# Moving two operand splits between weight pairs 1 and 2, and two output tiles within the last weight pair, in a hybrid encoder step

## The chip, the cores and the metric

The kernel runs on 1 core of one Trainium2 chip. The metric is the device time in microseconds of one execution, lower is better. Times are the median of several runs, and one further execution was profiled.

## The reference, cut to what matters

One layer of a hybrid encoder is computed for 1024 prompt tokens and 64 sample tokens, T = 1088 in all, at width 1024:

```
h = RMSNorm(x);  [u | v_g | q | k | v | g] = h @ w_in
A = gMLP chunked spatial gating of u and v_g
B = sliding-window attention with ALiBi and sinks, 16 q heads, 4 kv heads
x = x + w_o( sigmoid(g_A) * (A @ w_pa) + sigmoid(g_B) * (B @ w_pb) )
x = x + w_down( gelu(causal_dwconv3(h2 @ w_up_gate)) * (h2 @ w_up_val) ),  h2 = RMSNorm(x)
y = RMSNorm_final(x)
```

Outputs are y for all tokens and the new cache rows. Everything is float32. Each float32 operand is split in two fp32r parts, high and low, and a product is three passes over them: high by high, high by low, low by high.

## The kernel before, in words

All big matrix products run through 64 **weight pairs** p = 0 to 63 (two column tiles of 128 columns each, all 8 K-tiles), and what is left of w_down through a last part of its own. The moving operand, the activations, lies in SBUF as four quadrants (even or odd K-tiles, first or second 544 tokens). A pair is either **plain**, 8 products of quadrants, or a **Strassen-like** pair of 7 products on sums of quadrants. Pairs 0 and 1 are plain, pair 2 is the first with 7 products. One product is 4 K-tiles j by 3 passes by 2 halves of 272 tokens, 24 matmuls (line 2395).

The operands of the sums are numbered: 0, 1, 6 and 7 are the quadrants, 2, 3, 4 and 5 are sums. The plain pairs use 0, 1, 7 and 6; pair 2 uses 0 to 6 in that order, so operand 4 is first needed by its product k = 4 and operand 5 by k = 5. An operand is **split** in two steps: ScalarE writes `op_hi`, a copy of all 128x2176 elements rounded to fp32r (`operand_hi`, line 1288), and VectorE writes `op_lo`, the source less the high part (`operand_lo`, line 1730). In the first generation of operands (g = 0) operand 4's high part goes over the source of operand 5, so `operand_hi(0, 4)` waits until `op_lo` of 5 has been written.

Weights are treated alike: `raw` (one buffer) holds the pair's weights as loaded, ScalarE writes `w_hi` (line 1249), VectorE `w_lo` (line 1686), and in a 7-product pair VectorE first makes four sums of blocks (`weight_sum`, lines 1697, 1702, 1706, 1710). The order in which VectorE makes the low parts of pair 2 is places 3, 0, 1, 4 in pair 1 and, at the start of pair 2, the ones `left_over`: 2, 5, 6.

What is done when is written out by hand. Every engine runs the same loop over (p, k, j), product k of pair p and its K-tile j, and in each step issues what tables say belongs there. In a plain pair the product k has a slot number n: k = 0, 1, 3, 4, 5, 6, 7 is n = 0 to 6 and k = 2 has none; tables with (n, j) go by that. In a 7-product pair n = k. Engines wait for one another by semaphores and each works its own list strictly in order. The steps around the change, in the order of the lists:

- ScalarE, pair 1, k = 7 (n = 6), j = 0: copy of a finished quadrant out of PSUM, copy of v (`values(1)`, line 1345), then `operands` (line 1288), then the high part of pair 2's weight place 1; j = 1: that of place 4. Pair 2, k = 0, j = 0: the last quadrant of pair 1, high parts of places 2, 5, 6; j = 1: operand 5's high part (before); j = 3: `load_weights(act, 3)`; k = 1, j = 0: `copied(2, 0)`, which takes the first product of pair 2 out of PSUM into `m1c` (line 1336); then `values(2)` and, before, operand 4's high part.
- `load_weights(engine, p)` (line 613) issues two DMAs into `raw` and first waits for `s_w >= LOWS_BEFORE[p]`: for p = 3 that is until VectorE has made all low parts of pairs 0 to 2, since these read `raw`.
- VectorE, pair 1, k = 7: low part of place 1, the distance table (lines 1932 to 1936), low part of place 4, the fourth weight sum (line 1710, at j = 2). Pair 2, k = 0, j = 0: low parts of places 2, 5, 6; j = 2: operand 5's low part (before); k = 1, j = 2: operand 4's low part; k = 2: `combine(2, Q11)`.
- TensorE starts product k = 2 of pair 2 only when `copied(2, 0)` is done, since it writes the same PSUM region.

The last part of w_down works on 3 chunks of tokens: 512, 384 and 192 of them (`CHUNKS`), and 8 column tiles kt each, 6 matmuls per tile (line 2660). VectorE adds each to the residual (line 2308). Once a chunk is summed, its token tiles n (0 to 3, 4 to 6, 7 and 8) are **turned**: 8 transposes on TensorE (line 2642) into one of two PSUM places used in turn, a sum of squares on ScalarE (line 1653), the factor on GpSimd (lines 1117, 1120), and then **scaled** on VectorE into the output rows (line 2298), which SyncE stores. Tile n's transposes wait until tile n - 2 is scaled (tiles 2 to 6), those of tiles 7 and 8 until the third chunk is summed. `TURNS[c]` says behind which kt of chunk c TensorE turns a tile, `SCALES[c]` behind which kt VectorE scales one. A matmul group kt of the last two chunks waits for the addition four groups earlier, whose bank it takes.

Of the kernel before, what the change touches and what calls it, by code (L numbers as in the profile page):

```python
# [121 lines left out]

GROUPS = FT // 2 - 4 * NCHUNK
CHUNKS = ((0, 4), (4, 7), (7, NT))
TURNS = ({}, {1: 0, 3: 1, 5: 2, 7: 3}, {1: 4, 4: 5, 7: 6})

SCALES = ({}, {3: 0, 5: 1, 7: 2}, {2: 3, 5: 4, 7: 5})
BEFORE_LAST = 8 * (GROUPS - 1)


# [166 lines left out]
def program(nc, x_prompt, x_sample, cache_k, cache_v, cache_conv, ln_mix_g, w_in, ln_v_g, ln_v_b, w_s, b_s,  # L297
# [3 lines left out]
    with ExitStack() as ctx:  # L301
# [924 lines left out]
        def _(act):  # L1226
# [286 lines left out]
            def operands(p, n, j):  # L1513

                todo = ()
                for g in range(5, GENS):
                    if p == FIRST_PAIR[g] - 1:
                        todo = {(4, 2): (0,), (5, 2): (1,)}.get((n, j), ())
                    if p == FIRST_PAIR[g]:
                        todo = {(0, 2): (7,), (1, 2): (6,), (4, 2): (2,), (5, 2): (3,), (6, 2): (5,), (6, 3): (4,)}.get((n, j), ())  # L1520
                    for m in todo:
                        operand_hi(g, m, "w")
                    todo = ()
                for g in range(5):
                    if g and p == FIRST_PAIR[g] - 1:
                        if g < 3:
                            todo = {(2, 3): ((1, "w"),), (4, 0): ((0, "w"),), (5, 2): ((7, "w"),)}.get((n, j), ())
                        elif g == 3:
                            todo = {(1, 2): ((0, "a"),), (2, 2): ((1, "a"),), (5, 2): ((0, "b"),)}.get((n, j), ())
                        else:  # L1530
                            todo = {(1, 2): ((0, "a"),), (2, 0): ((3, "a"),), (2, 2): ((1, "a"),), (3, 2): ((0, "b"),),
                                    (5, 0): ((7, "a"),), (6, 2): ((1, "b"),)}.get((n, j), ())
                    if g and p == FIRST_PAIR[g]:
                        if g == 2:
                            todo = {(0, 2): ((6, "w"),), (1, 1): ((3, "w"),), (2, 0): ((2, "w"),), (3, 0): ((5, "w"),),
                                    (5, 0): ((4, "w"),)}.get((n, j), ())
                        elif g < 3:
                            todo = {(0, 2): ((6, "w"),), (1, 1): ((3, "w"),), (2, 0): ((2, "w"),), (4, 0): ((5, "w"),),
                                    (5, 0): ((4, "w"),)}.get((n, j), ())
                        elif g == 3:  # L1540
                            todo = {(0, 1): ((1, "b"),), (0, 2): ((7, "a"),), (1, 0): ((6, "a"), (6, "b")), (2, 0): ((7, "b"),)}.get((n, j), ())
                        else:
                            todo = {(0, 2): ((7, "b"),), (1, 0): ((6, "a"), (6, "b")), (2, 1): ((3, "b"),),
                                    (3, 0): ((2, "w"),), (4, 0): ((5, "w"),), (5, 0): ((4, "w"),)}.get((n, j), ())
                    if (p, g) == (1, 0):
                        todo = {(2, 2): ((3, "w"),), (5, 0): ((2, "w"),)}.get((n, j), ())
                    if (p, g) == (2, 0):
                        todo = {(0, 1): ((5, "w"),), (1, 0): ((4, "w"),)}.get((n, j), ())
# [109 lines left out]
        def _(dve):  # L1658
# [435 lines left out]
            def operands(p, n, j):  # L2094

                for g in range(5, GENS):
                    lows = ()
# [4 lines left out]
                    if p == FIRST_PAIR[g] + 1:  # L2102
                        lows = {(0, 3): (4,)}.get((n, j), ())
                    for m in lows:
                        operand_lo(g, m, "w")
                for g in range(5):
                    sums, lows = {}, {}
                    if g and p == FIRST_PAIR[g] - 1:
                        if g < 3:
                            sums = {(4, 3): ((0, "w"),)} if g == 1 else {(4, 3): ((0, "w"),), (5, 2): ((1, "w"),)}  # L2110
                            lows = {(3, 0): ((1, "w"),), (5, 1): ((0, "w"),), (6, 1): ((7, "w"),)}
                        elif g == 3:
                            lows = {(1, 3): ((0, "a"),), (2, 3): ((1, "a"),), (6, 1): ((0, "b"),)}
                        else:
                            sums = {(0, 3): ((0, "a"),), (1, 1): ((1, "a"),)}
                            lows = {(1, 3): ((0, "a"),), (2, 1): ((3, "a"),), (2, 3): ((1, "a"),), (3, 3): ((0, "b"),), (6, 1): ((7, "a"),),
                                    (6, 3): ((1, "b"),)}
                    if p == FIRST_PAIR[g]:
                        if g == 0:
                            sums = {(6, 2): ((0, "w"),)}  # L2120
                        elif g == 2:
                            sums = {(0, 2): ((2, "w"),), (1, 0): ((3, "w"),)}
                            lows = {(0, 3): ((6, "w"),), (1, 2): ((3, "w"),), (2, 0): ((2, "w"),), (3, 1): ((5, "w"),)}
                        elif g < 3:
                            sums = {(0, 1): ((1, "w"),), (1, 0): ((3, "w"),), (2, 2): ((2, "w"),)}
                            lows = {(1, 2): ((6, "w"),), (2, 0): ((3, "w"),), (3, 0): ((2, "w"),)}
                        elif g == 3:
                            lows = {(0, 2): ((1, "b"),), (1, 0): ((7, "a"),), (1, 2): ((6, "a"), (6, "b")), (2, 1): ((7, "b"),)}
                        else:
                            sums = {(2, 0): ((0, "b"), (1, "b")), (3, 0): ((2, "w"), (3, "w"))}  # L2130
                            lows = {(0, 3): ((7, "b"),), (1, 2): ((6, "a"), (6, "b")), (2, 2): ((3, "b"),),
                                    (3, 2): ((2, "w"),), (4, 2): ((5, "w"),), (5, 2): ((4, "w"),)}
                    if (p, g) == (1, 0):
                        sums = {(0, 2): ((1, "w"),), (1, 1): ((3, "w"),), (2, 3): ((2, "w"),)}
                        lows = {(3, 2): ((3, "w"),), (5, 2): ((2, "w"),)}
                    if g < 3 and p == lead(g) + 1 and summed(g):
                        lows = {(0, 2): ((4, "w"),)} if g == 2 else {(0, 2): ((5, "w"),), (1, 2): ((4, "w"),)}
# [555 lines left out]
```

## Time and profile before

| | us |
|---|---|
| median of 3 runs | 1627.47 (1627.44 to 1630.19) |
| the profiled execution's own time | 1628.09 |
| its span | 1626.3 |
| TensorE busy with matmuls | 1607.0 (99%) |
| VectorE busy | 1141.3 (70%) |
| ScalarE busy | 711.0 (44%) |

The span is what the profiler sees between the first and the last instruction or transfer. Matmul records overlap, so their busy time counts more than the array's work; idle times between them are real. Start times are us from the span's start.

### The profile page before, as it was taken

The numbers are of one execution on the slowest core, as the hardware profiler recorded it, in microseconds if no ns is written. First come the engines' busy times: TensorE is split into PE (matmuls) and PEld (weight loads), VectorE is DVE, ScalarE is ACT, GpSimd is POOL, SyncE is SP. The second block draws the span as 40 slices with busy tenths as digits, with TensorE's granted clock in tenths as the row PEclk, the third lists the DMA queues.
The fourth block names the chain that finished last, engine by engine and source line by source line (L and its number), as shares of the span: only waits on it lengthen the run. The fifth ranks groups of instructions, "written<-read, shape, count | busy, mean of one in ns | idle before, by whom it ended". The sixth has DMA issues, their size and how long they took to land.

```text
span 1626.3 us, 32456 instructions
## 1 busy us (share of the span) xinstructions
PE 1607.0 (99%) x12909; PEld 1571.6 (97%) x12909; DVE 1141.3 (70%) x2028; ACT 711.0 (44%) x1310; POOL 76.1 (5%) x145
## 2 busy tenths in 40 slices
PE   8999999999999999999999999999999999999997
PEld 8999899999999999999999999999999999999997
DVE  7666565656567869696625888888888776757566
ACT  8434454454444436463434534433343345434312
POOL 2000000000001000001112100000000000100001
PEclk9999999999999999999999999999999999999999
DMA  9354343443437774746742233333323227566312
GB/s 289 123 166 139 101 128 113 118 132 107 142 96 233 220 224 163 250 141 158 174 142 95 60 110 105 108 107 108 100 97 100 80 81 265 135 205 180 105 71 112
DMA packets 272490, 227.05 MB, mean 140 GB/s; under 512 B 43343, under 2 KB 223379, under 8 KB 272339
## 3 DMA queue, kind: packets, MB, share of 16 engines
q1 hardware_dynamic: 137891, 149.98, 27.6%
q10 hardware_dynamic: 131056, 66.07, 14.5%
q0 software_dynamic: 3392, 8.91, 3.2%
q8 instruction: 103, 1.69, 0.4%
q14 instruction: 48, 0.39, 0.1%
HBM read 150.56 MB, written 74.36 MB: 138 GB/s over the span
## 4 chain that ended last, share of the span: by engine, by line
PE 92%; DVE 3%; DMA 3%; issue 1%; ACT 1%; SPq 0%; ACTq 0%; POOLq 0%; DVEq 0%; POOL 0%
PE ps L2395 80%; PE ps L2623 3%; PE ps L2485 2%; PE ps L2660 1%; PE ps L2515 1%; PE ps L2543 1%; DVE op_lo L1730 1%; PE ps L2503 1%; PE ps L2520 1%; DMA raw<-in_w_in_dram 1%; DMA raw<-in_w_pa_dram 1%; DVE w_lo L1686 1%; DMA xt<-in_x_prompt_dram 1%; PE ps L2533 0%; PE ps L2505 0%
## 5 line engine op out<-in xcount | busy, mean ns | idle before, releaser
L2395 PE MATMUL ps<-op_hi,w_hi 128*128 128x272 f32 x3672 | 770.6, 291 | 4.4 <-DVE r L1851 1.4
L2395 PE MATMUL ps<-op_hi,w_lo 128*128 128x272 f32 x3672 | 759.5, 288 | 0.0
L2395 PE MATMUL ps<-op_lo,w_hi 128*128 128x272 f32 x3672 | 757.2, 288 | 0.0
L2395 PEld LDWEIGHTS ps<-op_hi,w_hi 128*128 128x128 f32 x3672 | 575.4, 188 | 15.6 <-issue 12.9
L2395 PEld LDWEIGHTS ps<-op_lo,w_hi 128*128 128x128 f32 x3672 | 576.8, 188 | 0.0
L2395 PEld LDWEIGHTS ps<-op_hi,w_lo 128*128 128x128 f32 x3672 | 573.5, 189 | 0.0
L1686 DVE TENSOR_TENSOR w_lo<-raw,w_hi 128x512 fp32r<-128x512 f32 x256 | 173.9, 698 | 161.0 <-ACT w_hi L1249 160.8
L1249 ACT ACTIVATE w_hi<-raw 128x512 fp32r<-128x512 f32 x256 | 153.6, 625 | 127.9 <-PE ps L2395 83.3
L1336 ACT ACTIVATE u<-ps 128x544 f32<-128x544 f32 x106 | 66.0, 623 | 227.1 <-PE ps L2395 227.1
L1249 ACT ACTIVATE w_hi<-w_f 128x512 fp32r<-128x512 f32 x159 | 95.5, 626 | 36.2 <-DVE w_f L1706 22.0
L1686 DVE TENSOR_TENSOR w_lo<-w_f,w_hi 128x512 fp32r<-128x512 f32 x159 | 105.0, 685 | 8.0 <-ACT w_hi L1249 7.5
L1361 ACT ACTIVATE sc_sb<-sc_sb,att_stat 128x192 f32<-128x192 f32 (+2 forms) x136 | 58.9, 435 | 51.7 <-DVE att_stat L1971 51.6
L1730 DVE TENSOR_TENSOR op_lo<-lo_f,op_hi 128x2176 fp32r<-128x2176 f32 (+2 forms) x31 | 72.6, 2345 | 12.2 <-ACT op_hi L1288 12.2
L1288 ACT ACTIVATE op_hi<-lo_f 128x2176 fp32r<-128x2176 f32 (+2 forms) x31 | 60.6, 1961 | 34.6 <-DMA lo_f<-g_spill 16.0
L1851 DVE TENSOR_TENSOR quad<-u,ps 128x544 f32<-128x544 f32 x69 | 49.4, 716 | 28.3 <-ACT u L1336 17.0
L1336 ACT ACTIVATE m1c<-ps 128x544 f32<-128x544 f32 x53 | 32.6, 615 | 59.9 <-PE ps L2395 34.7
L1730 DVE TENSOR_TENSOR op_lo<-r,op_hi 128x2176 fp32r<-128x2176 f32 (+2 forms) x25 | 42.7, 1722 | 12.6 <-ACT op_hi L1288 12.5
L2065 DVE SCALAR_TENSOR_TENSOR conv<-a_ext,conv_w,conv 128x1090 f32<-128x1090 f32 x22 | 29.8, 1354 | 29.5 <-ACT conv L1489 29.5
L1851 DVE TENSOR_TENSOR quad<-m1c,ps 128x544 f32<-128x544 f32 x23 | 16.6, 720 | 46.5 <-PE ps L2395 45.3
L1386 ACT ACTIVATE o_sb<-ps 128x256 f32<-128x256 f32 x32 | 12.3, 384 | 82.7 <-PE ps L2520 60.0
L1965 DVE CUSTOM_DVE_ANT_0 sc_sb<-ps,bias,sinks 128x192 f32<-128x192 f32 (+2 forms) x136 | 47.1, 401 | 0.3 <-issue 0.3
L1489 ACT ACTIVATE conv<-a_ext,consts,conv_w 128x1090 f32<-128x1090 f32 x22 | 28.6, 1302 | 42.2 <-issue 40.0
(208 smaller groups left out, 1529.1 us busy)
## 6 DMA issues: line engine op xcount, KB each, us to landing
in_spill<-quad SPq DMA_DIRECT2D x88, 272.0 KB, 2.2
raw<-in_w_up_dram ACTq DMA_DIRECT2D x44, 512.0 KB, 4.7
raw<-in_w_in_dram ACTq DMA_DIRECT2D x42, 512.0 KB, 5.4
g_spill<-value_out SPq DMA_DIRECT2D x22, 544.0 KB, 2.7
t_spill<-t_buf SPq DMA_DIRECT2D x8, 1088.0 KB, 4.4
lo_f<-g_spill SPq DMA_DIRECT2D x8, 1088.0 KB, 5.7
lo_f<-t_spill SPq DMA_DIRECT2D x8, 1088.0 KB, 6.6
raw<-in_w_down_dram ACTq DMA_DIRECT2D x16, 512.0 KB, 5.1
```

The costliest lines, as they stand in the source:

```text
L1249: act.activation(w_hi[n][:], weight_source(p, n), copy).then_inc(s_w_hi, 1)
L1288: act.activation(op_hi[at][:, j], operand_source(g, n)[:, j], copy).then_inc(s_op_hi, 1)
L1336: act.activation(two((m1c, u2, u3)[i][:]), reg[0][:, :, 0:HB], copy).then_inc(s_copied, 1)
L1361: act.activation(x, x, ACT.Exp, bias=a[:, 1, e:e + 1], accum_out=a[:, 3, e:e + 1])
L1686: dve.tensor_tensor(w_lo[n][:], weight_source(p, n), w_hi[n][:].bitcast(F32), ALU.subtract).then_inc(s_w, 1)
L1730: dve.tensor_tensor(op_lo[at][:, j], operand_source(g, n)[:, j], op_hi[at][:, j].bitcast(F32), ALU.subtract).then_inc(s_op, 1)
L1851: dve.tensor_tensor(two(out), two(first[:]), reg[region][:, :, 0:HB], op).then_inc(s_comb, 1)
L1965: last = dve.tensor_tensor_reduce(sc_sb[:, i % 2, h, columns_of(n, c)], side[:, h, columns_of(n, c)], bias[:, h, seen(n, c):SPAN], HD ** - ...
L2065: dve.scalar_tensor_tensor(cv, a_ext[:, 1:EXT - 1], conv_w[:, 1, f:f + 1], cv, ALU.mult, ALU.add).then_inc(s_c1, 1)
L2395: last = pe.matmul(out[:, h, 0:HB], (w_hi, w_lo)[a][place][:, j, :], (op_hi, op_lo)[b][at][:, j, HB * h:HB * h + HB], start=fresh and j == ...
L2485: last = pe.matmul(side[:, h, SPAN * c + w0:SPAN * c + SPAN], q_now[64 * h:64 * h + 64, s, c, :], k_now[64 * h:64 * h + 64, s, CHUNK * c + ...
L2623: last = pe.matmul(pset[t % 2][:, blkn, 0:t1 - t0], (d_hi, d_lo)[x][:, blk % 2, 512 * k + P * q:512 * k + P * q + P], (g_hi, g_lo)[y][g % ...
```

## The change

Operand 5's high part moves on ScalarE from pair 2, k = 0, j = 1 to pair 1, k = 7, j = 0, and its low part on VectorE from pair 2, k = 0, j = 2 to pair 1, k = 7, j = 3. Operand 4's high part moves from j = 0 to j = 1 of pair 2's k = 1 (its low part keeps its step, j = 2 of the same product). In the last chunk TensorE turns tile 5 behind kt = 3 instead of 4 and tile 6 behind 6 instead of 7; VectorE scales tile 3 behind kt = 1 instead of 2, tile 4 behind 4 instead of 5 and tile 5 behind 6 instead of 7. No instruction is added or taken away.

```diff
-TURNS = ({}, {1: 0, 3: 1, 5: 2, 7: 3}, {1: 4, 4: 5, 7: 6})
-
-SCALES = ({}, {3: 0, 5: 1, 7: 2}, {2: 3, 5: 4, 7: 5})
+TURNS = ({}, {1: 0, 3: 1, 5: 2, 7: 3}, {1: 4, 3: 5, 6: 6})
+
+SCALES = ({}, {3: 0, 5: 1, 7: 2}, {1: 3, 4: 4, 6: 5})
...
                     if (p, g) == (1, 0):
-                        todo = {(2, 2): ((3, "w"),), (5, 0): ((2, "w"),)}.get((n, j), ())
+                        todo = {(2, 2): ((3, "w"),), (5, 0): ((2, "w"),), (6, 0): ((5, "w"),)}.get((n, j), ())
                     if (p, g) == (2, 0):
-                        todo = {(0, 1): ((5, "w"),), (1, 0): ((4, "w"),)}.get((n, j), ())
+                        todo = {(1, 1): ((4, "w"),)}.get((n, j), ())
...
                     if (p, g) == (1, 0):
                         sums = {(0, 2): ((1, "w"),), (1, 1): ((3, "w"),), (2, 3): ((2, "w"),)}
-                        lows = {(3, 2): ((3, "w"),), (5, 2): ((2, "w"),)}
+                        lows = {(3, 2): ((3, "w"),), (5, 2): ((2, "w"),), (6, 3): ((5, "w"),)}
                     if g < 3 and p == lead(g) + 1 and summed(g):
-                        lows = {(0, 2): ((4, "w"),)} if g == 2 else {(0, 2): ((5, "w"),), (1, 2): ((4, "w"),)}
+                        lows = {(0, 2): ((4, "w"),)} if g == 2 else {(1, 2): ((4, "w"),)} if g == 0 else {(0, 2): ((5, "w"),), (1, 2): ((4, "w"),)}
```

## Rows read from the trace of the kernel before

**Rows 1.** The page: busy time by engine, granted clock, chain by engine.
```profile
PE 1607.0 (99%) x12909; PEld 1571.6 (97%) x12909; DVE 1141.3 (70%) x2028; ACT 711.0 (44%) x1310; POOL 76.1 (5%) x145
```
...
PEclk9999999999999999999999999999999999999999
...
PE 92%; DVE 3%; DMA 3%; issue 1%; ACT 1%; SPq 0%; ACTq 0%; POOLq 0%; DVEq 0%; POOL 0%
```

**Rows 2.** The waits of TensorE, whole run: us in total, times, longest.
```profile
PE ps L2395 <- ACT m1c L1336: 0.6, 1, 0.6
...
PE ps L2642 <- DVE y_sb L2298: 0.8, 2, 0.4
```

**Rows 3.** TensorE's timeline, end of pair 2's second product: start, duration, engine, line.
```profile
81.66 0.41 PE L2395 MATMUL ps<-op_hi,w_lo 128*128 128x272 f32 x2
82.67 0.49 PE L2395 MATMUL ps<-op_hi,w_hi 128*128 128x272 f32 x2 [0.59 <-ACT m1c L1336]
```

**Rows 4.** ScalarE's timeline, end of pair 1 and pair 2.
```profile
73.78 0.62 ACT L1249 ACTIVATE w_hi<-raw 128x512 fp32r<-128x512 f32 x1
...
79.37 2.01 ACT L1288 ACTIVATE op_hi<-hi_f 128x2176 fp32r<-128x2176 f32 x1
80.77 1.01 ACTq L613 DMA_DIRECT2D raw<-in_w_in_dram  x2
81.90 0.62 ACT L1336 ACTIVATE m1c<-ps 128x544 f32<-128x544 f32 x1 [0.53 <-issue]
...
83.95 2.02 ACT L1288 ACTIVATE op_hi<-lo_f 128x2176 fp32r<-128x2176 f32 x1 [1.16 <-DVE op_lo L1730]
...
100.24 1.14 ACTq L613 DMA_DIRECT2D raw<-in_w_in_dram  x2
```

**Rows 5.** VectorE's timeline of the same stretch.
```profile
75.99 0.68 DVE L1686 TENSOR_TENSOR w_lo<-raw,w_hi 128x512 fp32r<-128x512 f32 x1
...
78.05 0.68 DVE L1710 TENSOR_TENSOR raw<-raw,w_f 128x512 f32<-128x512 f32 x1
78.84 0.69 DVE L1686 TENSOR_TENSOR w_lo<-w_f,w_hi 128x512 fp32r<-128x512 f32 x1
79.45 1.29 DVE L1686 TENSOR_TENSOR w_lo<-raw,w_hi 128x512 fp32r<-128x512 f32 x2
81.41 2.43 DVE L1730 TENSOR_TENSOR op_lo<-hi_f,op_hi 128x2176 fp32r<-128x2176 f32 x1 [0.67 <-ACT op_hi L1288]
86.01 2.42 DVE L1730 TENSOR_TENSOR op_lo<-lo_f,op_hi 128x2176 fp32r<-128x2176 f32 x1 [2.17 <-ACT op_hi L1288]
88.35 0.71 DVE L1851 TENSOR_TENSOR quad<-m1c,ps 128x544 f32<-128x544 f32 x1
...
99.53 0.68 DVE L1686 TENSOR_TENSOR w_lo<-raw,w_hi 128x512 fp32r<-128x512 f32 x1
```

**Rows 6.** The timeline of the last chunk, all engines.
```profile
1609.58 0.54 POOL L1120 TENSOR_TENSOR stat_y<-stat_y,columns 128x1 f32<-128x1 f32 x1
...
1610.02 0.34 PE L2660 MATMUL ps<-g_hi,d_hi 128*128 128x192 f32 x1
...
1611.23 1.28 DVE L2298 SCALAR_TENSOR_TENSOR y_sb<-ps,stat_y,fin_g 128x1024 f32<-128x1024 f32 x1
...
1611.98 0.28 PE L2660 MATMUL ps<-g_hi,d_lo 128*128 128x192 f32 x1
...
1612.65 1.07 PE L2642 MATMUL ps<-ident,xy 128*128 128x128 f32 x8 [0.40 <-DVE y_sb L2298]
...
1613.47 0.34 PE L2660 MATMUL ps<-g_hi,d_hi 128*128 128x192 f32 x1
...
1614.40 0.36 DVE L2308 TENSOR_TENSOR xy<-ps,xy 128x192 f32<-128x192 f32 x1 [1.37 <-PE ps L2660]
...
1616.10 2.81 PE L2642 MATMUL ps<-ident,xy 128*128 128x128 f32 x24 [0.40 <-DVE y_sb L2298]
...
1618.41 1.02 ACT L1653 ACTIVATE y_junk<-ps 128x1024 f32<-128x1024 f32 x1
...
1619.25 3.68 DVE L2298 SCALAR_TENSOR_TENSOR y_sb<-ps,stat_y,fin_g 128x1024 f32<-128x1024 f32 x3 [1.58 <-POOL stat_y L1120]
```

**Rows 7.** Windows at the end: length, busy us by engine, granted clock, DMA share.
```profile
1622.00:1624.00 2.00, 0.00 (x0) 0.00 (x0) 0.93 (x1) 0.00 (x0) 0.00 (x0) 0.98 0.99 397
```

## The prediction

> **What bounds the kernel now.** I read the page first, then TensorE's waits, then the chain and the timelines of the two places that the change touches. TensorE is busy for 99% of the span at full granted clock and makes 92% of the chain of waits [rows 1]. So whatever is worth anything must come out of TensorE's few idle stretches or out of what follows its last instruction. In the whole run it waited for `m1c` on ScalarE once, 0.59 us, and for `y_sb` on VectorE twice, 0.8 us together [rows 2]. The first is the start of product k = 2 of pair 2, at 82.67 [rows 3]; the other two are the transposes of tiles 5 and 6, at 1612.65 and 1616.10 [rows 6]. These are the stretches that the change can shorten: 1.4 us at most, of 1626.3.
>
> What holds `m1c` at 81.90? ScalarE finished operand 5's high part at 79.37 + 2.01 = 81.38, and one would blame that. But the profile puts the last 0.53 us down to issue, and the two DMA issues of pair 3's weights run from 80.77 to 81.78 [rows 4]: the copy starts 0.12 behind them. The issues in turn start 0.03 after VectorE's last low part of pair 2 (79.45 + 1.29 = 80.74) [rows 5], which is what their semaphore asks for, as `raw` is free only then. The next pair shows the same: low part to 99.53 + 0.68 = 100.21 [rows 5], issues from 100.24 [rows 4]. So the chain into the 0.59 us is VectorE's low parts of places 2, 5, 6, then the refill's issue, then `m1c`, then TensorE.
>
> **The start, step by step.** (a) Operand 5's high part on ScalarE takes the slot at 73.78 of the high part of weight place 1 [rows 4]. Nothing else holds it, the sum that it reads having been made earlier in pair 1. It issues no DMA. 73.78 + 2.01 = 75.79, then place 1's high part, 0.62, to 76.41. VectorE's low part of place 1 started at 75.99 [rows 5] and now starts at about 76.35 (records of one engine overlap by up to 0.1): +0.36. Place 4's high part, one further on ScalarE, is ready before VectorE asks for it.
>
> (b) From 75.99 to the fourth weight sum at 78.05 [rows 5] VectorE's list is unchanged and dense, so the sum starts at 78.41.
>
> (c) Behind the sum stands the new step, operand 5's low part, which does not wait: its high part is there since 75.8. Before, the low part of place 2 came 78.84 - 78.05 = 0.79 after the sum. Now there are one 0.61 (78.84 to 79.45, the step between starts for this size) and one 2.34 (86.01 to 88.35) between them [rows 5]: 2.95 instead of 0.79, +2.16. The low part of place 2 starts at 78.84 + 0.36 + 2.16 = 81.36, the last of the three ends at 80.74 + 2.52 = 83.26.
>
> (d) ScalarE's list no longer has 2.01 us of operand 5 in pair 2, but stands at the refill's wait until 83.26. Queued behind it are `copied(2, 0)`, `values(2)` and operand 4's high part; TensorE waits for the first. Issues 83.29 to 84.30, `m1c` at 84.42, and TensorE's k = 2 at 84.42 + (82.67 - 81.90) = 85.19. That is 2.5 us later than before. The place where operand 5 was on VectorE, from 81.41 [rows 5], becomes idle time there: it had been after the refill's release, and now it is ahead of it. Moving the split early thus buys nothing and puts 2.3 us of VectorE in front of the only thing that was on the path.
>
> (e) Operand 4: ScalarE's high part before waited for operand 5's low part (1.16 us, to 83.95) [rows 4], and no longer does; it comes behind `m1c` and `values(2)`, no earlier than 85.0 and no later than 83.95 + 2.52 = 86.5. Its low part then ends between 1.1 and 2.5 later than the 88.43 of before [rows 5], while TensorE's k = 4 is 2.5 later. As TensorE did not wait there before, it does not now. `combine(2, Q11)`, behind it at 88.35, is later by no more than that too. The later step j = 1 costs nothing.
>
> (f) Pair 3's weights are asked for 2.5 us later, at the same distance from TensorE as before, and SyncE's stores and loads of pairs 2 and 3 follow TensorE and ScalarE. I found no wait behind this place that goes by the clock on the wall rather than by TensorE's progress, so the 2.5 us are kept to the end. Bounds for the start: if VectorE's wait before place 1 is hidden, 2.1; if the DMA issues stretch beside other traffic, up to 0.5 more, as the next pair's took 1.14 for 1.01 [rows 4]. So 2.1 to 3.1, taken 2.5.
>
> **The end, step by step.** Tile 3's factor is ready at 1609.58 + 0.54 = 1610.12 and its scaling ran at 1611.23 [rows 6]; behind kt = 1 it can run at about 1610.16, to 1611.43. TensorE's kt = 2, 3, 4 took 1610.02 to 1612.0, about 0.67 each [rows 6]. Behind kt = 3, at 1611.36, tile 5's transposes wait for the scaling plus 0.14 (before: 1612.51 to 1612.65): 1611.57. A turning takes 0.82 of TensorE (1612.65 to 1613.47), so kt = 4 starts at 1612.39 and its addition 0.93 later (1613.47 to 1614.40) [rows 6], 1613.32. Scaling of tile 4 at 1613.60, to 1614.87; tile 6's transposes at 1615.01, against 1616.10: 1.1 sooner. But now kt = 7 stands behind them: it starts at 1615.83, its addition is at 1616.76 to 1617.1, and tiles 7 and 8, which wait for that addition, start turning at 1617.25, where before they started at 1616.10 + 0.87 = 1616.97 [rows 6]. That is 0.28 later. ScalarE's squares took tile 7 at 1618.41 [rows 6], held back by tile 6's, 1.2 each; now tile 7's comes 1.10 behind its turning, at 1618.35, and tile 8's 1.2 after it. The end of the three last scalings, 1619.25 + 3.68 = 1622.93 [rows 6], becomes 1622.87. Of the 0.8 us of waiting saved on TensorE 0.06 is left, since the last tiles are limited by the last addition and by ScalarE. Tile 6's store leaves about 1 us sooner and may take a little load off the last ones. I take -0.1 for the end, with +0.4 and -0.5 as bounds (the one if the additions come a step later than I count, the other if the stores thin out).
>
> **The sum.** 1628.09 + 2.5 - 0.1 = 1630.5 for the profiled execution, which was 0.6 above the median; from the median, 1627.47 + 2.4 = 1629.9, 0.15% slower. What can be told from no change is about 0.2%, 3.3 us, so this counts as no change.
>
> **The rivals.**
> *A, the split is off the path and the stall goes.* `m1c` is held by operand 5's high part alone, the refill isn't on the path, and the 0.59 us close. For it: the chain passes through that ScalarE record. Against: the 0.12 and the 0.03 above. -0.6 - 0.1 gives 1626.8. Chance 0.10.
> *B, half.* VectorE takes the new step in slack that I don't see (the fourth sum or place 2 waits less), and 1.2 of the 2.5 show: 1628.6. Against it: the dense list in rows 5. Chance 0.06.
> *C, slower on the other side of 0.2%: the clock falls in the longer stall.* TensorE's idle time before 82.67 grows from 0.59 to about 3.1 us. At the end of the run the granted clock is still full for nearly all of the window to 1624 (mean 0.98) [rows 7], although TensorE's last record ended at 1618.91 [rows 6]: it had been idle for some 5 us when the clock fell. The stall is shorter than that, which speaks against. If the clock fell to 1.2 GHz all the same, and 5 us of matmuls ran so, half of them would be lost: 2.4 + 2.5 gives 1632.4. Chance 0.07. It decides with the length of the stall, so it gets likelier if (c) and (d) come out too short.
> The Trainium skill, "TensorE: Matmul & The Clock Gate", section "HAM oscillation", warns that a stall can cost more than its own length, since the array may run on at half rate behind it. By that rule the move is dearer than my sum; by the window of the trace it is not. No stretch of the run before has a stall of this length to decide it.
> *D, slower through the end.* kt = 7 and its addition behind tile 6 delay tiles 7 and 8 by more than ScalarE's slack, because the addition also stands behind the scaling of tile 5 on VectorE: if that scaling starts 0.5 later than the 1615.3 that I count, the addition is late by 0.4 and everything after it. With the start's upper bound: 3.1 + 0.6 gives 1631.2. Chance 0.07.
>
> **How the numbers follow.** My forecast has 0.70. Its own range is 1627.47 + 1.6 to + 3.5, 1629.1 to 1631.0. Slower by over 0.2% (above 1630.7): C and D, 0.14, and the upper tenth of my case, 0.07, 0.22 with the spread of the medians, of which one run before was 1630.19. Faster by over 0.2% no term reaches, 0.03 for what I have not seen. The same: 0.75. The range that holds 8 in 10 has to take in B and most of A below, and D above, and leaves C out: 1626.8 to 1631.6.
>
> **What would show it.** In TensorE's waits `m1c` stands with about 3.1 us instead of 0.6, and k = 2 of pair 2 starts near 85.2. VectorE's `op_lo <- hi_f` runs from about 79.0 to 81.4, directly followed by three low parts, and the two `raw` issues start 0.03 after the last, near 83.3. A high part of operand 5 stands at 73.8. Operand 4's low part ends before 91.0. The granted clock stays full at 85 to 95. In the last chunk tile 5's transposes stand 1.1 sooner relative to kt = 2, tile 6's too, and tile 7's not sooner. I am wrong in the main point if the issues start at 80.8 or if `m1c` does not follow them; wrong in its size if VectorE's sum at 78.4 or the step behind it is elsewhere; and wrong in (f) if the 2.5 us are no longer there in pair 3.

## The result and the profile after

| us | before | after |
|---|---|---|
| median (18 runs each) | 1629.47 (1626.95 to 1634.14) | 1632.9 (1629.45 to 1636.37) |
| profiled execution, span | 1628.09, 1626.3 | 1635.84, 1634.0 |

The ratio is 1.0021, 95% interval 1.0012 to 1.0031: 3.4 us slower, between 2.0 and 5.1. The forecast was 1629.9 in a range of 1626.8 to 1631.6, so it missed by 3.0: 2.0 us of that is that the kernel before itself has a median 2.0 us higher over 18 runs than over the 3 that were shown, and 1.0 us is in the difference (2.4 forecast, 3.4 measured).

Read the changed place first. ScalarE's timeline of the kernel after, to hold against [rows 4]:

```profile
73.89 2.02 ACT L1288 ACTIVATE op_hi<-hi_f 128x2176 fp32r<-128x2176 f32 x1
75.80 0.62 ACT L1249 ACTIVATE w_hi<-raw 128x512 fp32r<-128x512 f32 x1
...
83.38 1.01 ACTq L613 DMA_DIRECT2D raw<-in_w_in_dram  x2
84.51 0.62 ACT L1336 ACTIVATE m1c<-ps 128x544 f32<-128x544 f32 x1 [4.58 <-issue]
```

VectorE's, to hold against [rows 5]:

```profile
76.45 0.69 DVE L1686 TENSOR_TENSOR w_lo<-raw,w_hi 128x512 fp32r<-128x512 f32 x1 [0.27 <-ACT w_hi L1249]
...
78.52 0.69 DVE L1710 TENSOR_TENSOR raw<-raw,w_f 128x512 f32<-128x512 f32 x1
79.12 2.42 DVE L1730 TENSOR_TENSOR op_lo<-hi_f,op_hi 128x2176 fp32r<-128x2176 f32 x1
81.46 0.69 DVE L1686 TENSOR_TENSOR w_lo<-w_f,w_hi 128x512 fp32r<-128x512 f32 x1
82.06 1.29 DVE L1686 TENSOR_TENSOR w_lo<-raw,w_hi 128x512 fp32r<-128x512 f32 x2
...
87.34 2.42 DVE L1730 TENSOR_TENSOR op_lo<-lo_f,op_hi 128x2176 fp32r<-128x2176 f32 x1 [4.00 <-ACT op_hi L1288]
```

This trace runs 0.1 late from the start. With that, each stands where steps (a) to (d) put it: high part at 73.8, low part 79.0 to 81.4, refill 0.03 behind the last low part (82.06 + 1.29 = 83.35), `m1c` 0.12 behind the refill. TensorE's timeline, to hold against [rows 3], shows the longer stall and then something that my sum has not:

```profile
85.28 0.49 PE L2395 MATMUL ps<-op_hi,w_hi 128*128 128x272 f32 x2 [3.09 <-ACT m1c L1336]
...
87.07 0.65 PE L2395 MATMUL ps<-op_hi,w_hi 128*128 128x272 f32 x2
87.52 0.66 PE L2395 MATMUL ps<-op_lo,w_hi 128*128 128x272 f32 x2
...
90.14 0.41 PE L2395 MATMUL ps<-op_lo,w_hi 128*128 128x272 f32 x2
```

Two matmuls took 0.25 us from start to start in the stream before the stall, and here they take 0.45. The windows say why (length; busy PE, PEld, DVE, ACT, POOL; granted clock; DMA share; GB/s):

```profile
85.00:86.00 1.00, 0.72 (x6) 0.76 (x7) 0.00 (x0) 1.00 (x3) 0.00 (x0) 1.00 1.08 326
86.00:87.00 1.00, 1.00 (x9) 1.00 (x8) 0.00 (x0) 1.00 (x1) 0.00 (x0) 0.79 1.18 326
87.00:88.00 1.00, 1.00 (x7) 1.00 (x6) 0.66 (x1) 0.31 (x1) 0.00 (x0) 0.50 1.12 277
88.00:89.00 1.00, 1.00 (x6) 1.00 (x6) 1.00 (x1) 0.00 (x0) 0.00 (x0) 0.50 1.12 356
89.00:90.00 1.00, 1.00 (x6) 1.00 (x5) 1.00 (x2) 0.00 (x0) 0.00 (x0) 0.51 1.09 387
90.00:91.00 1.00, 1.00 (x9) 1.00 (x9) 0.40 (x1) 0.97 (x2) 0.00 (x0) 1.00 1.10 384
```

The granted clock is 0.50, which is 1.2 GHz, between 86.6 and 90.0. That is rival C.

TensorE's waits over the whole run, the two of [rows 2], a wait for a quadrant at 620 that is not the change's (below), and tile 7's wait for the last addition:

```profile
PE ps L2395 <- ACT m1c L1336: 3.1, 1, 3.1
PE ps L2395 <- DVE quad L1851: 2.7, 1, 2.7
...
PE ps L2642 <- DVE xy L2308: 0.5, 1, 0.5
PE ps L2642 <- DVE y_sb L2298: 0.4, 1, 0.4
```

And the last chunk, all engines, to hold against [rows 6]:

```profile
1617.98 1.29 DVE L2298 SCALAR_TENSOR_TENSOR y_sb<-ps,stat_y,fin_g 128x1024 f32<-128x1024 f32 x1 [0.37 <-POOL stat_y L1120]
...
1619.41 1.06 PE L2642 MATMUL ps<-ident,xy 128*128 128x128 f32 x8
...
1622.87 1.07 PE L2642 MATMUL ps<-ident,xy 128*128 128x128 f32 x8 [0.40 <-DVE y_sb L2298]
...
1624.62 0.36 DVE L2308 TENSOR_TENSOR xy<-ps,xy 128x192 f32<-128x192 f32 x1 [0.18 <-PE ps L2660]
...
1625.03 1.97 PE L2642 MATMUL ps<-ident,xy 128*128 128x128 f32 x16 [0.45 <-DVE xy L2308]
...
1626.16 1.02 ACT L1653 ACTIVATE y_junk<-ps 128x1024 f32<-128x1024 f32 x1 [1.08 <-PE ps L2642]
```

One wait on `y_sb` (tile 5's) is gone, and a wait of tile 7 for the last addition has taken its place. Between the square of tile 3 and the last scaling's end lie 14.82 us before and 14.75 after.

**Why the spans differ by 7.7 us.** Not all of it is the change's. I compare the copies out of PSUM (line 1336), one by one, at their times in the trace of before: after is 2.6 us late at `m1c`, 4.1 at the next copy, and but for one copy stays at 4.1 to 4.2 until 604. Then 2.7 come at 611, where a load of w_pb's weights landed after 13.8 us, and 1.1 between 922 and 929, behind a second fall of the clock; the rest is smaller steps of both signs. A second trace of the unchanged kernel (e9, below) differs from the first by as much at 611 and by 1.4 at 922.

### The profile page after: what moved, and what is told of

The parts are those of the page before. It is cut to its first block, busy times and chain, and to the rows that moved or that the text cites. A ratio compares the mean times of both kernels' runs of the same rounds, so it can differ in the third digit from the quotient of the medians.

```text
span 1634.0 us, 32456 instructions
## 1 busy us (share of the span) xinstructions
PE 1609.4 (98%) x12909; PEld 1573.9 (96%) x12909; DVE 1141.9 (70%) x2028; ACT 711.2 (44%) x1310; POOL 77.0 (5%) x145
## 4 chain that ended last, share of the span: by engine, by line
PE 91%; DVE 3%; DMA 3%; issue 2%; ACT 1%; SPq 0%; ACTq 0%; DVEq 0%; POOL 0%
PE ps L2395 79%; PE ps L2623 3%; PE ps L2485 2%; PE ps L2660 1%; PE ps L2515 1%; PE ps L2543 1%; PE ps L2503 1%; DMA raw<-in_w_pb_dram 1%; PE ps L2520 1%; DMA raw<-in_w_in_dram 1%; DMA raw<-in_w_pa_dram 1%; DVE w_lo L1686 1%; DVE op_lo L1730 1%; DMA xt<-in_x_prompt_dram 1%; PE ps L2533 0%
## 5 line engine op out<-in xcount | busy, mean ns | idle before, releaser
L2395 PE MATMUL ps<-op_hi,w_hi 128*128 128x272 f32 x3672 | 772.0, 292 | 9.4 <-ACT m1c L1336 3.1
L2395 PE MATMUL ps<-op_hi,w_lo 128*128 128x272 f32 x3672 | 761.5, 289 | 0.0
L2395 PE MATMUL ps<-op_lo,w_hi 128*128 128x272 f32 x3672 | 759.1, 288 | 0.0
L2395 PEld LDWEIGHTS ps<-op_hi,w_hi 128*128 128x128 f32 x3672 | 577.1, 189 | 20.5 <-issue 18.4
L2395 PEld LDWEIGHTS ps<-op_lo,w_hi 128*128 128x128 f32 x3672 | 578.6, 189 | 0.0
L2395 PEld LDWEIGHTS ps<-op_hi,w_lo 128*128 128x128 f32 x3672 | 575.3, 189 | 0.0
L1686 DVE TENSOR_TENSOR w_lo<-raw,w_hi 128x512 fp32r<-128x512 f32 x256 | 174.1, 699 | 164.8 <-ACT w_hi L1249 164.7
L1249 ACT ACTIVATE w_hi<-raw 128x512 fp32r<-128x512 f32 x256 | 153.6, 625 | 129.2 <-PE ps L2395 83.2
L1336 ACT ACTIVATE u<-ps 128x544 f32<-128x544 f32 x106 | 66.0, 623 | 229.4 <-PE ps L2395 229.2
L1686 DVE TENSOR_TENSOR w_lo<-w_f,w_hi 128x512 fp32r<-128x512 f32 x159 | 105.2, 686 | 8.2 <-ACT w_hi L1249 7.7
L1249 ACT ACTIVATE w_hi<-w_f 128x512 fp32r<-128x512 f32 x159 | 95.6, 626 | 35.0 <-DVE w_f L1706 20.2
L1730 DVE TENSOR_TENSOR op_lo<-lo_f,op_hi 128x2176 fp32r<-128x2176 f32 (+2 forms) x31 | 72.7, 2347 | 14.1 <-ACT op_hi L1288 14.1
L1288 ACT ACTIVATE op_hi<-lo_f 128x2176 fp32r<-128x2176 f32 (+2 forms) x31 | 60.7, 1962 | 32.8 <-DMA lo_f<-g_spill 15.7
L1851 DVE TENSOR_TENSOR quad<-u,ps 128x544 f32<-128x544 f32 x69 | 49.4, 717 | 28.9 <-ACT u L1336 17.6
L1336 ACT ACTIVATE m1c<-ps 128x544 f32<-128x544 f32 x53 | 32.6, 615 | 63.9 <-PE ps L2395 34.9
L1730 DVE TENSOR_TENSOR op_lo<-r,op_hi 128x2176 fp32r<-128x2176 f32 (+2 forms) x25 | 42.8, 1724 | 12.8 <-ACT op_hi L1288 12.7
L1851 DVE TENSOR_TENSOR quad<-m1c,ps 128x544 f32<-128x544 f32 x23 | 16.6, 721 | 46.5 <-PE ps L2395 45.3
```

Source lines behind the costliest of these rows:

```text
L1249: act.activation(w_hi[n][:], weight_source(p, n), copy).then_inc(s_w_hi, 1)
L1288: act.activation(op_hi[at][:, j], operand_source(g, n)[:, j], copy).then_inc(s_op_hi, 1)
L1336: act.activation(two((m1c, u2, u3)[i][:]), reg[0][:, :, 0:HB], copy).then_inc(s_copied, 1)
L1686: dve.tensor_tensor(w_lo[n][:], weight_source(p, n), w_hi[n][:].bitcast(F32), ALU.subtract).then_inc(s_w, 1)
L1730: dve.tensor_tensor(op_lo[at][:, j], operand_source(g, n)[:, j], op_hi[at][:, j].bitcast(F32), ALU.subtract).then_inc(s_op, 1)
L1851: dve.tensor_tensor(two(out), two(first[:]), reg[region][:, :, 0:HB], op).then_inc(s_comb, 1)
```

## The experiments

Two executions of one program differ here by up to 10 us (1624.34 to 1634.26 for the kernel before, in the 35 runs beside e5 to e8), and an interval over 12 runs is some 2 us to either side. The traces settle more: up to 590 us, times counted from ScalarE's first copy of v (line 1345, at 68.97 before) agree to 0.03 us between the two traces of the unchanged kernel (12.94 and 12.94 to `m1c`, 16.98 and 16.99 to pair 2's second copy). So the start is read as these distances, and the end as the distance from tile 3's square (line 1653) to the last scaling's end.

| distances in us | v to m1c | v to 2nd copy | v to 4th copy | last chunk | median, us | ratio to before, 95% |
|---|---|---|---|---|---|---|
| before | 12.94 | 16.98 | 32.66 | 14.82 | | |
| e9, before again | 12.94 | 16.99 | 32.69 | 14.81 | 1631.47 | 1.0003 (0.9991 to 1.0014) |
| after | 15.44 | 20.95 | 36.71 | 14.75 | 1632.9 | 1.0021 (1.0012 to 1.0031) |
| e1, start only | 15.41 | 20.99 | 36.69 | 14.82 | 1632.76 | 1.0022 (1.0010 to 1.0034) |
| e2, end only | 12.94 | 16.98 | 32.67 | 14.76 | 1627.87 | 1.0000 (0.9986 to 1.0015) |
| e3, stall filled | 15.43 | 19.48 | 35.17 | 14.82 | 1628.08 | 0.9999 (0.9989 to 1.0010) |
| e3b, half filled | 15.41 | 19.47 | 35.16 | 14.82 | 1630.25 | 0.9997 (0.9989 to 1.0006) |
| e4, low part back | 13.29 | 17.35 | 33.04 | 14.81 | 1629.3 | 1.0003 (0.9993 to 1.0014) |
| e5, e1 with the refill later | 10.76 | 16.44 | 32.93 | 14.82 | 1628.26 | 0.9993 (0.9984 to 1.0003) |
| e6, before with the refill later | 12.32 | 16.91 | 34.65 | 14.82 | 1630.75 | 1.0005 (0.9994 to 1.0016) |
| e7, another order of the end | 12.94 | 16.99 | 32.67 | 13.86 | 1628.69 | 0.9998 (0.9988 to 1.0009) |
| e8, e5 and e7's end | 10.76 | 16.44 | 33.48 | 13.86 | 1628.71 | 0.9993 (0.9983 to 1.0003) |
| e10, e4 with the refill behind m1c | 10.76 | 17.55 | 33.16 | 14.82 | 1631.14 | 1.0001 (0.9990 to 1.0013) |
| e11, e10 and e7's end | 10.77 | 17.81 | 33.43 | 13.85 | 1629.77 | 0.9993 (0.9983 to 1.0004) |
| e12, e4 with the distance table later, e7's end | 12.42 | 16.47 | 32.17 | 13.85 | 1629.07 | 0.9994 (0.9981 to 1.0007) |
| e13, e10 with the stores of v later, one run | 10.76 | 16.51 | 33.85 | 14.81 | 1630.79 | |

**e1_start and e2_tail: the two halves.** e1 is the changed kernel with these two tables as before; e2 has them as changed, and all else as before:

```diff
-TURNS = ({}, {1: 0, 3: 1, 5: 2, 7: 3}, {1: 4, 3: 5, 6: 6})
-SCALES = ({}, {3: 0, 5: 1, 7: 2}, {1: 3, 4: 4, 6: 5})
+TURNS = ({}, {1: 0, 3: 1, 5: 2, 7: 3}, {1: 4, 4: 5, 7: 6})
+SCALES = ({}, {3: 0, 5: 1, 7: 2}, {2: 3, 5: 4, 7: 5})
```

> Only the moves of operands 5 and 4, the last part as before. Theory (the new low part stands ahead of the refill's release, and the longer stall lets TensorE's clock fall): TensorE idle before product k = 2 of pair 2 about 3.1 us, the clock at half rate for about 3 us behind it, 96 matmuls from there in 13.8 us instead of 12.3, so +4.0 us against before, ratio 1.0025. Rival (the clock's fall was that one execution's, the stall alone counts): +2.5 us, ratio 1.0015, granted clock full at 86 to 90. Rival (the time comes from late weight loads further on, as at 601 to 615): no difference beyond noise and no clock fall.

> Only the moves in the last chunk. Theory: tile 6's transposes 1.1 us sooner, those of tile 7 0.2 to 0.3 later, last scaling ends less than 0.1 us sooner counted from tile 3's transposes (15.8 instead of 15.9 us); ratio 1.0000. Rival (the last chunk carries part of the loss): the last scaling ends 0.5 us or more later, ratio 1.0003 to 1.0008. Rival (the author's gain): 1.0 us sooner, 0.9994.

Both as the theory had it. All of the loss is in e1: +2.5 to `m1c`, +4.0 at the next copy, ratio 1.0022, and the clock at 0.55 and 0.60 from 86 to 90 in this execution too. None of its 12 runs, and none of the 18 of after, shows a mean granted clock above 0.998, where 14 of the 35 runs of before beside e1 show 0.999. Among the 16 traces only those without a fall before the last matmul show 0.999, so the fall is not that of the profiled executions alone. e2 gains 0.06 us in the last chunk.

**e3_warm and e3b_warm12: what brings the clock down.** e1 with work added to TensorE in the stall, turnings of a 128x128 tile whose results nobody reads (e3b: 12 in place of 24):

```diff
                     for j in range(4):
+                        if (p, k, j) == (2, 2, 0):
+                            for _ in range(24):
+                                pe.transpose(side[:, 1, 0:P], ident[:], ident[:])
                         product(p, k, j)
```

> The start change as in e1, and 24 transposes of the identity matrix, whose result nobody reads, on TensorE ahead of product k = 2 of pair 2, so that it has about 2.6 us of work in the stall. Theory: k = 2 starts at the same time as in e1 (about 85.2), the clock stays full, the 96 matmuls take 12.3 us: 1.5 us faster than e1, +2.5 against before. Rival (the half rate comes from something else than the idle stretch, say traffic of the refill at 84 to 91): half rate also here, same time as e1.

> As e3_warm with 12 transposes instead of 24, so that TensorE is idle for about 1.9 us ahead of k = 2 instead of 0.5 (e3) or 3.1 (e1). Theory (the idle time is what brings the clock down): full clock at 86 to 90, the 96 matmuls from k = 2 in 12.3 us, copies of pair 2's products as late as in e3: +2.5 us against before at the second, not +4.1. Rival (any longer idle time brings it down): half rate for 3.4 us as in e1.

TensorE's timeline of e3:

```profile
84.56 0.49 PE L2395 MATMUL ps<-op_hi,w_hi 128*128 128x272 f32 x2 [0.48 <-ACT m1c L1336]
```

And its windows, TensorE's clock being the eighth column as before:

```profile
86.00:88.00 2.00, 2.00 (x18) 2.00 (x17) 1.38 (x1) 0.75 (x2) 0.00 (x0) 1.00 1.09 311
88.00:90.00 2.00, 2.00 (x18) 2.00 (x17) 2.00 (x3) 1.53 (x3) 0.00 (x0) 1.00 1.09 387
```

`m1c` comes as late as in e1 (15.43), the refill's traffic is the same (1.09 DMA share), the clock stays full, and the second copy is at 19.48 instead of 20.99. The half rate thus costs 1.5 us and comes from the idle stretch. With 1.80 us idle it stays full too. Each of the two is one trace, but 9 of e3's 11 runs and 5 of e3b's 11 show a mean of 0.999, where none of e1's did. TensorE's timeline of e3b:

```profile
84.98 0.49 PE L2395 MATMUL ps<-op_hi,w_hi 128*128 128x272 f32 x2 [1.80 <-ACT m1c L1336]
```

The whole times don't fit as well: both have +2.5 at the start and ratios of 0.9999 and 0.9997, where 1.0015 was expected, outside both intervals. Part of it is that the clock fell less often later on. The mean granted clock over e3's runs is 0.9988 against 0.9980 for the runs of before beside it, in e3b 0.9983 against 0.9979. One stretch at half rate as above (3.4 us) takes 0.001 from the mean of a run and cost 1.5 us, so an estimate from these numbers is 1.2 us less for e3 and 0.5 for e3b. That leaves e3 inside its interval and e3b still outside. Why the clock should fall less often, and where the rest goes, I could not show; it stays open. The distances at the start are what shows the cost of the fall.

**e4_low_back: ScalarE's move or VectorE's?** e1 with this line as before:

```diff
-                        lows = {(3, 2): ((3, "w"),), (5, 2): ((2, "w"),), (6, 3): ((5, "w"),)}
+                        lows = {(3, 2): ((3, "w"),), (5, 2): ((2, "w"),)}
```

and operand 5's low part back at pair 2's k = 0, j = 2.

> Operand 5's high part early as in the change, its low part back at its old step behind the low parts of places 2, 5, 6. Theory (VectorE's low part ahead of the refill is the cause, ScalarE's move costs only the 0.36 of place 1): refill issued near 81.1, m1c near 82.3, stall 0.9 to 1.0 us, no clock fall, +0.3 us against before, ratio 1.0002. Rival (the early high part on ScalarE delays the chain): stall and loss as in e1, +4.0.

TensorE's timeline of e4:

```profile
83.00 0.49 PE L2395 MATMUL ps<-op_hi,w_hi 128*128 128x272 f32 x2 [0.95 <-ACT m1c L1336]
```

The stall is 0.95, `m1c` 0.35 late: the 0.36 of step (a). The other 2.12 of e1 (15.41 less 13.29, 2.16 in step (c)) are VectorE's low part.

**e5_refill_after, e6_refill_before: take the refill off the path.** In e1 and in the kernel before:

```diff
-                        if (k, j) == ((1, 2) if not plain(p) and plain(p - 1) and p > 2 else (2, 3) if p == 0 else (0, 3)) and p + 1 < NPAIR:
+                        if (k, j) == ((1, 2) if not plain(p) and plain(p - 1) else (2, 3) if p == 0 else (0, 3)) and p + 1 < NPAIR:
```

> The start change as in e1 (last part as before), and the refill for pair 3 issued at pair 2's k = 1, j = 2 instead of k = 0, j = 3, so behind the copy m1c in ScalarE's list, where the kernel has it for the later pairs of this kind. Theory (the refill's wait on VectorE's low parts is what holds m1c): m1c right behind product k = 0, near 79.2; k = 2 then waits only for the low part of place 2 (to about 82.1), stall under 0.3 us, no clock fall at 86; k = 2 starts near 82.1 to 82.3; 0.5 us faster than before, ratio 0.9997, and 4.5 us faster than e1. The refill comes 2.5 us later than before and hides. Rival (the late refill makes pair 3 late): a new stall at pair 3's first products, near 103. Rival (VectorE's extra low part delays TensorE by another way, place 2): stall of 1 us or more at 82.

> The kernel before, with the refill for pair 3 issued at pair 2's k = 1, j = 2 as in e5. Theory: m1c is then held by operand 5's high part only, to 81.4, and runs to 82.0; k = 2 starts 0.4 to 0.6 us sooner than before (near 82.2), ratio 0.9997. Rival (m1c is held by the high part as much as by the refill): k = 2 not before 82.6, no gain.

Right about `m1c` (2.18 and 0.62 sooner), wrong about the rest. In e6 TensorE's next waits are 1.54 for a quadrant and 0.84 for k, and ScalarE stands 6.42 us for the weights. TensorE's timeline of e6:

```profile
96.71 0.49 PE L2395 MATMUL ps<-op_hi,w_hi 128*128 128x272 f32 x2 [1.54 <-DVE quad L1851]
110.56 0.72 PE L2485 MATMUL ps<-k_now,q_now 64*128 64x64 f32 x8 [0.84 <-DMA k_now<-in_spill]
```

ScalarE's:

```profile
92.65 1.15 ACT L1249 ACTIVATE w_hi<-raw 128x512 fp32r<-128x512 f32 x2 [6.42 <-DMA raw<-in_w_in_dram]
```

The quadrants of pair 2 stand behind the high and low parts of pair 3's weights on both engines, so the refill has a due time in pair 2 that I had not seen. The rival of e5, that the late refill makes something late, holds, only sooner than it said. In e6 the start ends 2.6 us behind the kernel before (48.08 to 45.51, from the first copy of v to the sixth copy); in e5, where operands 4 and 5 are out of the way, it ends level (38.63 to 38.67 at the fifth copy), so that nothing of the 2.18 is left.

**e10_start_best, e13_stores_late: a collision.** e4 with the refill at (1, 0) of pair 2, behind `m1c` and ahead of operand 4:

```diff
-                        if (k, j) == ((1, 2) if not plain(p) and plain(p - 1) and p > 2 else (2, 3) if p == 0 else (0, 3)) and p + 1 < NPAIR:
+                        if (k, j) == ((1, 0) if p == 2 else (1, 2) if not plain(p) and plain(p - 1) else (2, 3) if p == 0 else (0, 3)) and p + 1 < NPAIR:
```

e13 has SyncE's stores of v later besides:

```diff
-                if (p, n, j) == (2, 1, 3):
+                if (p, n, j) == (2, 2, 3):
```

> Operand 5's high part early as in the change, its low part at its old step, and the refill for pair 3 at pair 2's k = 1, j = 0, behind m1c and ahead of operand 4's high part; last part as before. Theory: m1c at 79.3, no wait of TensorE on it; refill issued as before near 81.1, so no late weights as in e5 and e6; k = 2 starts near 82.0; 0.7 us faster than before, kept at pair 3 (milestone at 107 and after: -0.7), ratio 0.9996. Rival (operand 4's low part now ends just behind TensorE's arrival at k = 4): a stall of up to 0.3 us at 88. Rival (the refill at this place is late all the same): stalls at 95 as in e5.

> e10 with SyncE's stores of v (and the load of k behind them) issued behind its store of pair 2's first quadrant, at about 88 instead of 79, so that they don't run beside the refill's issue. Theory (the two issues of the refill took 3.34 us instead of 1.01, and its landing 10 us instead of 6, because they run beside these stores): issues take 1.0 to 1.1 us, no stall at k = 4 of pair 2 (1.11 us in e10), second copy of pair 2 0.5 to 0.7 us sooner than in the kernel before, counted from the copy of v; a stall may come at the transposes of k near 94, since their load is late. Rival (the refill is slow in this place for a reason of its own): issues take 3 us again and the 1.1 us of stall stay.

ScalarE's timeline of e10:

```profile
79.32 3.34 ACTq L613 DMA_DIRECT2D raw<-in_w_in_dram  x2
82.79 2.02 ACT L1288 ACTIVATE op_hi<-lo_f 128x2176 fp32r<-128x2176 f32 x1 [4.00 <-issue]
```

SyncE's queue of e10:

```profile
79.24 0.58 SPq L855 DMA_DIRECT2D vt_spill<-v_tok  x1
79.86 2.65 SPq L856 DMA_DIRECT2D out_dram<-v_tok  x1
```

ScalarE's timeline of e13:

```profile
80.78 1.01 ACTq L613 DMA_DIRECT2D raw<-in_w_in_dram  x2
...
83.19 2.02 ACT L1288 ACTIVATE op_hi<-lo_f 128x2176 fp32r<-128x2176 f32 x1 [2.95 <-DVE op_lo L1730]
```

TensorE's of e13:

```profile
95.57 0.63 PE L2469 MATMUL ps<-ident,k_in 128*128 128x128 f32 x4 [1.53 <-DMA k_in<-in_spill]
```

In e10 the two issues of the refill run beside the stores of v and hold ScalarE for 3.34 us, and operand 4's high part, operand 4's low part and TensorE's k = 4 (1.11 us idle) are late: e10 is 0.5 late at the fourth copy, where 0.7 sooner was expected. In e13, apart from the stores, the issues take 1.01 again and the 1.11 is gone, and the load of k that stands behind the moved stores costs 1.53 instead. The Trainium skill, "DMA: Bandwidth & Descriptors", section "Issuing engines are not separate DMA queues", says that transfers issued by several engines run on the same 16 DMA engines, and that only issue time is saved by it, which is usually small relative to the transfer. No run here tests the first by itself. As to the second, the issue time was 1.01 us in e13 and grew to 3.34 us in e10.

**e7_tail_best, e8_both, e11_best, e12_dist_late: what would be faster.** The last chunk of all four, against the change's:

```diff
-TURNS = ({}, {1: 0, 3: 1, 5: 2, 7: 3}, {1: 4, 3: 5, 6: 6})
-SCALES = ({}, {3: 0, 5: 1, 7: 2}, {1: 3, 4: 4, 6: 5})
+TURNS = ({}, {1: 0, 3: 1, 5: 2, 7: 3}, {1: 4, 3: 5, 7: 6})
+SCALES = ({}, {3: 0, 5: 1, 7: 2}, {1: 3, 4: 4, 7: 5})
```

> The kernel before with the last chunk at TURNS {1: 4, 3: 5, 7: 6} and SCALES {1: 3, 4: 4, 7: 5}: tile 5 is turned sooner as in the change, but tile 6 stays behind kt = 7, and tile 5's scaling stands behind the last addition. Theory (tiles 7 and 8 wait for the last addition, which the change put behind tile 6's transposes and tile 5's scaling): last addition near 0.8 us sooner than in the kernel before, from tile 3's transposes to the last scaling's end 14.9 us instead of 15.9, ratio 0.9994. Rival (ScalarE's squares or the output transfers set the end): no gain over 0.2 us.

> e5 and e7's last chunk together. Theory: 0.5 + 1.0 us faster than the kernel before, ratio 0.9991, and 5.5 us faster than the changed kernel, 0.9966 of it. Rival: the gains of e5 or e7 don't add up, since a stall further on takes the start's gain back; ratio 0.9994 or more.

> e10's start and e7's last chunk together. Theory: 0.7 us at the start and 0.96 in the last chunk (squares of tile 3 to the last scaling's end 13.86 instead of 14.82), together 1.7 us faster than before, ratio 0.9990, 5 us faster than the changed kernel. Rival: what is won at the start is lost at one of the late weight loads (604 to 611, 759 to 777), whose length differs from run to run; ratio 0.9995 or more.

e8 starts like e5 and e11 like e10. e12 starts like e4, with VectorE's distance table moved out of pair 1:

```diff
-                if (p, n, j) == (1, 6, 0):
+                if (p, n, j) == (2, 0, 3):
```

> e4 (high part early, low part at its old step, refill at its old step) with VectorE's distance table moved behind operand 5's low part, and e7's last chunk. Theory: the last low part of pair 2 ends 0.85 sooner than in e4, 0.5 sooner than in the kernel before; refill, m1c and k = 2 follow: m1c at 12.4 from the first copy of v instead of 12.94, kept in all later copies of pair 2 (16.5 instead of 16.98); last chunk 13.86 instead of 14.82. Together 1.5 us faster than before, ratio 0.9991. Rival: the refill, now sooner, still ends in a stall at k = 4 or 5, as e10's did: 0 or less won at the start.

TensorE's timeline of e7: the three turnings follow one another.

```profile
1616.31 2.79 PE L2642 MATMUL ps<-ident,xy 128*128 128x128 f32 x24
```

VectorE's: the last addition (in the group of three) now comes ahead of tile 5's scaling.

```profile
1615.96 0.91 DVE L2308 TENSOR_TENSOR xy<-ps,xy 128x192 f32<-128x192 f32 x3
1616.79 1.27 DVE L2298 SCALAR_TENSOR_TENSOR y_sb<-ps,stat_y,fin_g 128x1024 f32<-128x1024 f32 x1
```

The last chunk is 0.96 us shorter in all four (0.97 in two of them). ScalarE's timeline of e12:

```profile
80.26 1.01 ACTq L613 DMA_DIRECT2D raw<-in_w_in_dram  x2
81.39 0.62 ACT L1336 ACTIVATE m1c<-ps 128x544 f32<-128x544 f32 x1 [2.44 <-issue]
```

The 0.85 us taken from VectorE ahead of the refill brought `m1c` from e4's 13.29 to 12.42 (12.4 was forecast) and the second copy to 16.47 (16.5): the chain of step (d) works in both directions. In the two places that it touches e12 takes 1.5 us less than the kernel before (0.5 at the start, 0.97 at the end). e8 and e11 have `m1c` 2.2 sooner and lose it again: e8 is 0.8 late at the fourth copy, e11 0.8 there and 1.3 later on (46.81 to 45.51), so only their tails are left. Whole times don't prove a gain in any of the four: their ratios are 0.9993 to 0.9998 where 0.9990 to 0.9994 was expected, and each interval holds 1.

**e9_before_again: what is not the change's.**

> The kernel before unchanged, for a second trace of it. It shows which of the later differences between the two traces belong to the change: theory, none of those behind pair 2 (stall of 0 to 2.7 us at 604 to 620, 0 to 2.7 at 759 to 777, half rate near 909 or not): at least one of them differs here too from the first trace of before, by 1 us or more. Rival: this trace agrees with the first within 0.5 us at every milestone, and the later differences are the change's.

Its trace ends 5.8 us later than the first one of before: among the steps are 2.3 more at 611, 1.1 at 644, 1.4 at 922, 2.2 at 1477 and 1.1 at 1504, and 1.9 less at 767. The weight load in its chain of waits:

```profile
597.31 13.41 DMA raw<-in_w_pb_dram
```

The window behind it:

```profile
615.00:620.00 5.00, 4.19 (x21) 4.22 (x22) 5.00 (x6) 2.26 (x2) 0.00 (x0) 0.66 0.82 315
```

TensorE stood 2.34 us there before it began again at 615.8. So late weights at 611 and half rate behind a stall happen without the change.

## Why the prediction was right or wrong

- **What bounds the start, (a) to (d): right, shown.** +2.5 at `m1c`, stall 3.09 us for 3.1. e4 against e1 splits it into 0.35 and 2.12 for 0.36 and 2.16, and e12 runs the chain backwards.
- **(e), operand 4: right.** Its low part ended at 89.76, and TensorE's only wait in pair 2 is the one on `m1c`.
- **(f), kept to the end: right up to 600 us.** Behind that the weight loads differ from run to run by more than the change, and the whole times of e3 and e3b do not show the 2.5. The step had no term for the clock.
- **Rival C's chance, 0.07: this is what failed.** The sum has the stall at its own length and the clock's fall behind it at nothing. The clock did fall, and cost 1.5 us (e1 against e3), which is more than the 1.0 that the difference lacks: 2.5 + 1.5 - 0.1 = 3.9, in the measured 2.0 to 5.1. I read the end of the run [rows 7] as if TensorE had to be idle for the 5.0 us that passed between the last matmul's end at 1618.9 and the fall at 1623.9. In the trace of after the fall comes at 86.6, 4.4 us after TensorE went idle at 82.2, but TensorE had been at work again since 85.28: 3.1 us of idle had been enough. The delay of the clock's answer was taken for the length of its cause. Nor is that delay always 5 us: at the end of after the last transposes end at 1627.0 and the clock falls 2.4 later,

```profile
1629.00:1631.00 2.00, 0.00 (x0) 0.00 (x0) 1.68 (x2) 0.00 (x0) 0.36 (x1) 0.60 0.53 217
```

  and over the 16 traces it is 2.2 (e5) to 5.1 (e8). The price, 2.5, was too high by 1.0: the prediction took 5 us at half rate, for which it had no row, and it was 3.4. The rule of the Trainium skill, "TensorE: Matmul & The Clock Gate", section "HAM oscillation", that a stall can cost more than its own length, spoke against the change, and e1 and e3 bear it out. I had weighed it below the row, and the row said less than I took from it.
- **The end: right, shown.** Counted from tile 3's square, tile 6 is sooner by 1.05, tile 7's square by 0.07, and the whole by 0.07 for 0.06. e7 shows what takes the gain back: the last addition behind tile 6's turning and tile 5's scaling. It moves both, so their shares are not known.
- **Rivals A, B and D: refuted** by `m1c` at 15.44, by e4's 0.35 and 2.12, and by e2.
- **The range** was built on a median of three runs; the same kernel moved 2.0 us with 18. The bounds of the terms had no part for that. On the median that was shown, the measured terms give 1627.47 + 3.9 = 1631.4, just inside the range; on the median of 18 the forecast's own 2.4 gives 1631.9, just outside.

## What to carry to other kernels

When a step is moved earlier, look at what it now stands ahead of: here 2.3 us of VectorE's work went from behind a release (the weight buffer's) to ahead of it, and 2.1 of it arrived on TensorE. A stall that grows can cost more than it grows by, because the clock may fall behind it; the time at which the clock falls after the last matmul of a run says nothing about how short a stall may bring it down, and filler work on the idle engine is a cheap test, in more than one trace, since stalls of 2.3 to 2.8 us did it in two traces and not in six others. When tiles are finished sooner in a tail, put the addition on which the last ones wait ahead of the scalings, or the gain ends there.

## What the runs showed of the hardware that I had not expected

- TensorE's clock went to 1.2 GHz behind a stall of 3.1 us in both traces that have one (after, e1) and stayed at 2.4 behind stalls of 1.8 (e3b), 0.95 (e4) and 0.5 (e3). It fell 1.3 us after the work had begun again in after, 0.9 in e1.
- Between them the length of the stall alone does not decide. Of the eight stalls of 2.3 to 2.8 us in the 16 traces (seven between 612 and 621 us, e1's at 772), two brought the clock down: 2.34 us in e9 and 2.69 in e1. Six did not: 2.43 (e8), 2.44 (e10), 2.60 (e7), 2.73 (after), 2.74 (e13) and 2.78 (e12). The changed kernel, TensorE's timeline and a window behind the stall, the clock full:

```profile
620.17 0.49 PE L2395 MATMUL ps<-op_hi,w_hi 128*128 128x272 f32 x2 [2.73 <-DVE quad L1851]
...
622.00:624.00 2.00, 2.00 (x18) 2.00 (x17) 2.00 (x4) 0.55 (x1) 0.00 (x0) 1.00 0.64 244
```

  And e1, where it fell:

```profile
774.56 0.49 PE L2395 MATMUL ps<-op_hi,w_hi 128*128 128x272 f32 x2 [2.69 <-DVE r L1851]
...
775.00:777.00 2.00, 2.00 (x14) 2.00 (x13) 2.00 (x5) 1.15 (x2) 0.45 (x1) 0.67 0.00 0
```

  What else decides no run here tests.
- It also fell without any such stall, in 6 of the 16 traces, between 899 and 910 us, 2.2 to 3.4 us after the first of 18 matmuls of one column each (line 2551). These stand in every trace; that they are the reason is not tested. The kernel after (columns of the window as above):

```profile
906.14 2.05 PE L2551 MATMUL ps<-columns,gate_out 128*128 128x1 f32 x18
...
910.00:915.00 5.00, 5.00 (x32) 5.00 (x32) 5.00 (x5) 3.24 (x5) 0.52 (x1) 0.74 0.00 0
```

  TensorE counts as 100% busy there and is at three quarters of its clock on average: 32 matmuls in 5 us instead of the 43 that the kernel before has in the same window.
- Two DMA issues on ScalarE took 1.01 us apart from SyncE's issues of the stores of v (before, e13) and 3.34 us beside them (e10). What in the stores does it is not tested.
